# A hybrid decoder layer on one core: the state's chain ahead of the fourth attention block in the mixing stage

## What is computed

```python
h = rmsnorm(x, attn_norm_w); p = h @ w_in
q, k, v, p_rw = split(p)                      # 4 attention heads, 8 recurrent heads of 64
s = rope(q) @ rope(k).T * scale, causal       # two maps c for each attention head
p = softmax(s); a = p[0] - lam * p[1]
o_da = rmsnorm(a @ v, subln_w) * (1 - lam_init)
# recurrent group, state st of 64 x 64 for each head:
st = st * w_t - (st @ kk_t) * (kk_t * a_t) + v_t * k_t ;  y_t = st @ r_t
o_rw = (groupnorm(y) + bonus) * g
x = x + concat(o_da, o_rw) @ w_out
x = x + moe(rmsnorm(x))                       # top 4 of 32 experts, clamped SwiGLU
out = rmsnorm(x, final_norm_w)
```

## Time and profile before

| | |
|---|---|
| median of 3 runs | 1608.11 us (1607.88 to 1608.6) |
| the profiled execution's own time | 1607.04 us |
| its span | 1605.3 us |
| TensorE busy | 1544.0 us (96%) |
| VectorE busy | 1320.3 us (82%) |
| ScalarE busy | 1068.9 us (67%) |
| GpSimd busy | 324.7 us (20%) |
| DMA | 465.30 MB, mean 290 GB/s |

### The profile page before, as it was taken

One profiled execution on the slowest core, in us unless ns is written; L12 is line 12 of the kernel. 1 busy time (PEld: TensorE's weight loads), 2 busy tenths in 40 slices (PEclk: granted clock), 3 DMA queues, 4 the chain that ended last, 5 costly groups with the idle time before them and its releaser, 6 DMA issues.

```text
span 1605.3 us, 27281 instructions
## 1 busy us (share of the span) xinstructions
PE 1544.0 (96%) x10197; PEld 1253.3 (78%) x10198; DVE 1320.3 (82%) x1098; ACT 1068.9 (67%) x1011; POOL 324.7 (20%) x278
## 2 busy tenths in 40 slices
PE   5999999987899999999999999999999999999996
PEld 4777777765778888888888888888888888888885
DVE  5556565656498999999999999999999999999996
ACT  4635353434367777777777777777777777777774
POOL 6300000000145321122212211221122112212210
PEclk9999999998999999999999999999999999999998
DMA  6211111005399999999999999999999999999992
GB/s 191 63 54 41 55 41 54 15 2 215 157 391 367 373 395 385 382 380 374 376 372 381 388 384 374 376 367 376 373 386 382 379 373 376 371 371 381 381 377 114
DMA packets 98957, 465.30 MB, mean 290 GB/s; under 512 B 11392, under 2 KB 38048, under 8 KB 49616
## 3 DMA queue, kind: packets, MB, share of 16 engines
q1 hardware_dynamic: 86032, 429.59, 68.5%
q0 software_dynamic: 12864, 34.85, 8.3%
HBM read 448.51 MB, written 22.69 MB: 294 GB/s over the span
## 4 chain that ended last, share of the span: by engine, by line
PE 74%; DVE 1%; DMA 1%; issue 0%; ACT 0%; DVEq 0%; POOLq 0%
PE psum L1926 29%; PE psum L1929 14%; PE psum L1954 14%; PE psum L1959 7%; PE psum L1324 3%; PE psum L1908 2%; PE psum L1916 2%; PE psum L1942 1%; DVE w_pieces_lo L1748 0%; DMA xg<-h_rows,gath_i 0%; PE psum L2044 0%; PE psum L1340 0%; PE psum L1332 0%; DVE x L1870 0%; DMA w_pieces<-in_w_out 0%
## 5 line engine op out<-in xcount | busy, mean ns | idle before, releaser
L1748 DVE TENSOR_TENSOR w_pieces_lo<-w_pieces,w_pieces_hi 128x2048 fp32r<-128x2048 f32 x384 | 867.2, 2286 | 80.0 <-ACT w_pieces_hi L1612 79.9
L1612 ACT ACTIVATE w_pieces_hi<-w_pieces 128x2048 fp32r<-128x2048 f32 x384 | 736.1, 1919 | 220.4 <-PE psum L1929 156.3
L1926 PE MATMUL psum<-w_pieces_hi,xh 128*128 128x512 f32 x1024 | 284.4, 399 | 0.0
L1926 PE MATMUL psum<-w_pieces_hi,xl 128*128 128x512 f32 x1024 | 274.4, 390 | 0.0
L1929 PE MATMUL psum<-w_pieces_lo,xh 128*128 128x512 f32 x1024 | 274.2, 389 | 0.0
L1926 PEld LDWEIGHTS psum<-w_pieces_hi,xl 128*128 128x128 f32 x1024 | 192.2, 188 | 41.3
L1929 PEld LDWEIGHTS psum<-w_pieces_lo,xh 128*128 128x128 f32 x1024 | 192.2, 188 | 40.2
L1926 PEld LDWEIGHTS psum<-w_pieces_hi,xh 128*128 128x128 f32 x1024 | 185.4, 189 | 45.1 <-issue 11.3
L1552 POOL DMA_INDIRECT sum_rows<-ys,this_i x30 | 106.1, 3537 | 421.0 <-ACT ys L1632 420.7
L1954 PE MATMUL psum<-w_pieces_hi,ah 128*128 128x512 f32 x512 | 158.0, 390 | 0.1
L1954 PE MATMUL psum<-w_pieces_hi,al 128*128 128x512 f32 x512 | 157.7, 389 | 0.0
(11 more groups left out here) (366 smaller groups left out, 1893.2 us busy)
## 6 DMA issues: line engine op xcount, KB each, us to landing
w_pieces<-in_mlp_w SPq DMA_DIRECT2D x384, 1024.0 KB, 8.2
w_raw<-in_w_in SPq DMA_DIRECT2D x26, 512.0 KB, 4.0
w_pieces<-in_w_out SPq DMA_DIRECT2D x8, 512.0 KB, 9.3
sum_rows<-x POOLq DMA_DIRECT2D x5, 512.0 KB, 3.7
chunk_work<-in_x SPq DMA_DIRECT2D x4, 512.0 KB, 5.7
sc<-pall POOLq DMA_DIRECT2D x16, 128.0 KB, 3.8
x<-in_x SPq DMA_DIRECT2D x4, 512.0 KB, 13.8
h_rows<-w_pieces POOLq DMA_DIRECT2D x4, 512.0 KB, 2.9
```

The costliest lines, as they stand in the source:

```text
L1612: nc.scalar.activation(hi[:, p % RING], raw[:, raw_slot(b, p)].rearrange("p r n -> p (r n)"), ACT.Copy).then_inc(s_hi, 1)
L1748: nc.vector.tensor_tensor(lo[:, p % RING], raw[:, raw_slot(b, p)].rearrange("p r n -> p (r n)"), hi[:, p % RING].bitcast(F32), ALU.subtrac ...
L1926: nc.tensor.matmul(bank(up_bank(b) + c), a[:, k, :], hi[:, p % RING, c * 512:(c + 1) * 512], start=False, stop=False)
```

## The change

Three streams are reordered, and the three lists of names with them. Nothing is added and nothing is left out.

- ScalarE: `exponents(3)` comes behind the two copies e_wu0 and e_wu1 rather than ahead of them.
- VectorE: `weights(3)` comes behind z1 rather than ahead of L743.
- TensorE: `turn_weights(3)` comes behind `state(1)` and `y_within(0)` rather than ahead of them, and `output(3)` comes behind `state(3)` rather than ahead of `y_within(2)`.

```diff
--- before.py
+++ after.py
@@ -197,10 +197,10 @@
           + ["t2_0", "t2_1", "mr", "x2_0", "a_turn0", "x2_1", "o0", "score1"]
           + ["t3_0", "t3_1", "t_khat", "bonus", "x3_0", "a_turn1", "x3_1", "o1", "score2"]
           + ["t4_0", "t4_1", "t_v", "x4_0", "a_turn2", "x4_1", "o2", "akv", "score3"]
-          + ["wu0", "wu1", "q", "chunk", "a_turn3", "z1", "z2", "o3", "z3", "z4", "z5", "y_in", "z6", "o_turn", "y", "y_sum"])
+          + ["wu0", "wu1", "q", "chunk", "z1", "a_turn3", "z2", "z3", "o3", "z4", "z5", "y_in", "z6", "o_turn", "y", "y_sum"])
 MIX_ACT = (["sig_w", "kk_sq", "sig_a", "exps", "kk_log", "kk_norm", "grow", "keep", "gate", "e_kappa", "e_beta"]
            + ["exp0", "v_major", "a_major0", "o_copy0", "exp1", "e_khat", "a_major1", "o_copy1", "exp2", "e_v", "a_major2", "o_copy2"]
-           + ["e_akv", "exp3", "e_wu0", "e_wu1", "a_major3", "o_copy3", "o_log", "o_rs", "o_n", "gain", "y_sq", "y_log", "y_rs"])
+           + ["e_akv", "e_wu0", "e_wu1", "exp3", "a_major3", "o_copy3", "o_log", "o_rs", "o_n", "gain", "y_sq", "y_log", "y_rs"])
 MIX_DVE = (["mix_k", "kk0", "lsum", "mix_r", "mix_v", "kk",
             "kappa", "b", "beta", "rhat", "kmod", "khat"]
            + [f"{a}{h}" for h in range(2) for a in ("x1a", "x1b", "ea")]
@@ -208,7 +208,7 @@
               "ek0", "ek1", "max0"]
            + [n for lv in range(2, 5) for n in [f"et{lv}_0", f"et{lv}_1"] + [f"{a}{lv - 2}" for a in ("rl", "nl", "a")]
               + [f"ex{lv}_0", f"ex{lv}_1"] + [[], [], ["er"], ["bon", "shade"], []][lv] + [f"max{lv - 1}"]]
-           + ["rl3", "nl3", "a3", "eg", "eh", "e_q"] + [f"z{c}" for c in range(1, 8)]
+           + ["eg", "eh", "e_q", "z1", "rl3", "nl3", "a3"] + [f"z{c}" for c in range(2, 8)]
            + ["o_out", "y_n", "ot1", "ot2"])
 
 
@@ -511,10 +511,10 @@
             act.wait_ge(PE.sem, PE.reached(j, "akv"))
             nc.scalar.activation(rh[:, :, :, 64:128].rearrange("p h t c -> p (h t) c"),
                                  bank(2).rearrange("p (u c) -> p u c", c=64), ACT.Copy).then_inc(AC.sem, AC.step("e_akv"))
-            exponents(3)
             for h in range(2):
                 act.wait_ge(PE.sem, PE.reached(j, f"wu{h}"))
                 nc.scalar.activation(wu[:, h].rearrange("p t c -> p (t c)"), bank(3 * (1 - h)), ACT.Copy).then_inc(AC.sem, AC.step(f"e_wu{h}"))
+            exponents(3)
             weights_turned(3)
             output_copied(3)
             act.wait_ge(AC.sem, AC.reached(j, f"o_copy{NT - 1}"))
@@ -737,7 +737,6 @@
             largest(3)
             if more:
                 split(n0 + 6)
-            weights(3)
 
             dve.wait_ge(PE.sem, PE.reached(j, "chunk"))
             nc.vector.tensor_tensor(gt[:].rearrange("p (t c) k -> p c t k", c=2), psum[:, 0:2, 0:256].rearrange("p c (t k) -> p c t k", k=64),
@@ -752,6 +751,7 @@
                                     kr[:, :, 1, :].rearrange("p t (c k) -> p c t k", c=2), ALU.add).then_inc(DV.sem, DV.step("e_q"))
             own("eh")
             nc.vector.tensor_copy(zz[:, 1, :], hp[:, 0, :]).then_inc(DV.sem, DV.step("z1"))
+            weights(3)
             for c in range(1, 7):
                 dve.wait_ge(PE.sem, PE.reached(j, f"z{c}"))
                 nc.vector.scalar_tensor_tensor(zz[:, c + 1, :], bank(2, c * 64, c * 64 + 64), pe_[:, c, CH:CH + 1],
@@ -987,7 +987,6 @@
                                             start=False, stop=True)
             last.then_inc(PE.sem, PE.step("chunk"))
             fill(n0 + 4, 6, 8)
-            turn_weights(3)
 
             def y_within(u):
 
@@ -1008,11 +1007,12 @@
 
             state(1)
             y_within(0)
+            turn_weights(3)
             state(2)
             y_within(1)
-            output(3)
             y_within(2)
             state(3)
+            output(3)
             y_within(3)
             y_within(4)
             state(4)
```

## The result

The changed kernel takes 1612.3 us, the median of 16 runs (1610.51 to 1613.7), against 1607.98 us for the kernel before (16 runs): a ratio of 1.0026, with a 95% interval of 1.0019 to 1.0033. That is 4.3 us slower, over the 0.2% that can be told from no change. The forecast was 3.0 us slower, at 1611.1 us, with a range from 1607.9 to 1612.8. The profiled execution took 1610.51 us at a span of 1608.8, the fastest of the 16.

The account below looks back on a forecast made before the run. TensorE was taken to bound the kernel, 74% of the span, with the end of `front` passing delays on one to one. 3 x 0.91 + 0.30 = 3.0 us gave 1611.1 us from 1608.11, range 1607.9 to 1612.8.

Parts of the forecast that it names:

- forecast proper: Whole kernel: 3.0 us slower, own range 1610.3 to 1612.0 from 0.78 to 1.1 per turn and 0.1 to 0.5 in turn 4; chance 0.6.
- rival B: Turns 1 to 3: each pays unhidden tiling changes, 0.37 a turn, 1.1 in three; 4.1 us slower, 1612.2; chance 0.2.
- 373.2 foretold: Sign at the end of `front`: output projection loads (L1116) issued near 373.2, against 370.18 before.
- `q` earlier by 1.17 in turn 4: ScalarE's part in turn 4: with `wu` copied ahead of the exponentials, `q` starts at about 352.31 instead of 353.48.
- No gain in turns 1 to 3: ScalarE's part there brings nothing, since `q` starts behind tile slices after the last copy ends; z1 does not move.
- `am` 1.30 behind z1's start: VectorE's `weights(3)` between z1 and z2: `am` ready 1.30 us after z1's start, TensorE waiting and going on 0.06 later.
- 0.91 for each of turns 1 to 3: TensorE's part: state(4) starts 0.91 us later in each of turns 1 to 3, 2.7 in all.
- Nothing hides it: Next turn starts from y_sum behind 18 tile matmuls on TensorE, so the delay of turns 1 to 3 is passed on whole.
- +0.30 in turn 4: End of turn 4: the attention block, ready early before, becomes the late one; output(3) and y come 0.30 us later.
- 0.58 that I had used: TensorE's four transposes plus the way back to 64 x 64 pieces, ahead of state(2): 0.58 us.
- C: Absorbed: next turn waits for something not hanging on TensorE, giving back 0.91 per turn; only +0.30 stays, 1608.4; chance 0.13.
- A: Faster: the wait for `am` holds nobody, turns 1 to 3 cost nothing, turn 4 gives 1.17; 1606.9 us; chance 0.07.

Follow-up runs that it names:

- e1: The change made in turn 4 alone, turns 1 to 3 as in the kernel before: 1608.36 us against 1608.43 for the kernel before.
- e11: The kernel with the change in turn 4 alone, profiled a second time, one run: 1607.9 us.
- e3: The changed kernel plus ten idle-filling matmuls in TensorE's waits of turn 4: 1609.87 us against 1608.43 for the kernel before.
- e4: Only TensorE's order changed against the kernel before, ScalarE and VectorE left as they were: 1609.69 us against 1608.43.
- e6: Only ScalarE's order changed against the kernel before, copies of wu ahead of the exponentials: 1606.97 us against 1608.19.
- e9: The changed kernel unaltered, run for a third profile, one execution: 3120 us.
- e8: The kernel before plus five filling matmuls behind the transposes of turn 4: 1607.94 us against 1608.19 for the kernel before.
- e10: The changed kernel unaltered, run for a fourth profile, one run: 1612.04 us.
- e5: The changed kernel unaltered, measured again with a second profile: 1613.2 us against 1608.19 for the kernel before.

## Why the forecast came out as it did

The measured 1612.3 us lies in the stated range, but above the 1610.3 to 1612.0 of the forecast proper, and "slower by over 0.2%", which is what came, had the smaller chance (0.4 against 0.57 for no difference that can be told). The mechanism of the sum was right and gives 2.6 us; that the range held the rest too is luck, since it was stretched for rival B, and the term that filled it was in no rival. L1116 at 373.00 against the 373.2 foretold is luck as well: 1.7 us less ahead of the first `wu` and 1.9 more by turn 4's clock met there.

- **`q` earlier by 1.17 in turn 4**: right, 1.18. No gain in turns 1 to 3: right, z1 stands where it stood.
- **`am` 1.30 behind z1's start, and TensorE held by it**: right to 0.01. The transposes start 8.80 behind L967 in turn 1 (8.81 foretold), state(2) 9.38 (9.39), state(3) 10.10 (10.11), `output(3)` 10.37 (10.37).
- **0.91 for each of turns 1 to 3**: the mechanism was right and one term mis-sized, the two y_within behind `output(3)`. I took 0.4 from a stretch that held a wait; state(4) follows the output's end (124.80) by about 0.28. So the turn costs 0.78. Three of them: 2.3 instead of 2.7.
- **Nothing hides it**: right, the distances from y to the next `wu` are unchanged.
- **+0.30 in turn 4, since the attention block becomes the late one**: right where the clock holds, 13.98 and 13.97 (e1, e11, e3) against 13.67.
- **What failed** is a term that the sum did not have: TensorE's clock in turn 4. I costed the two waits there (2.1 us before the first state, 0.5 before the transposes) at their own length, because TensorE had nothing else to do. The turn cost up to 1.9 us more (15.83 against 13.98), through a clock of 0.50 in the stretch behind them, and filling them took that away (e3).
- **Rival B** (4.1 us) had the right size for the wrong reason: its changes of form would have shown as 1.28 in each of turns 1 to 3, and those took 0.78, of which e4 leaves 0.15 for the order. The drain at a change of tiling mode that the Trainium skill names (TensorEngine Tiling (Array Packing), Key Properties) was inside the 0.58 that I had used: state(2) came where it was foretold. **C** fell with the unchanged distances, **A** with the 0.56 that TensorE waits for `am`.

For the clock the Trainium skill has a rule, which I did not use: TensorE: Matmul & The Clock Gate, Part 1: The HAM clock gate, says that the array's clock is halved by default and that only activity lifts it. The fourth turn agrees in part: 0.50 behind idling and 1.00 in e3 with the same waits filled, but 1.00 too in e1 and e11 with the waits unfilled.

What stays open is why the same turn 4 lost its clock in three profiles of three in the changed kernel and in none of two in e1's. It starts 0.7 to 2.9 us earlier in e1's (`wu` at 349.57 and 349.37, against 350.30, 351.26 and 352.22), but the start alone doesn't decide: e4 and e6 lost the clock with `wu` at 349.42 and 349.65. Chance, with odds that differ from kernel to kernel, fits as well, and no run moved the new turn 4 alone. How many executions of the changed kernel lose the clock isn't known either. Their times, all 22 at 1610.5 us or more against a sum without it of about 1610.6, say that most do. The mean granted clock of each run points the same way: 0.9865 over these 22, and 0.9878 over e3's 11, which is 2.1 us of full clock less.

## What to carry to other kernels

Before an operation is moved into a chain of short round trips, look at what the chain's engines must do in order: VectorE's 1.2 us for the attention weights was free in its old place and became TensorE's wait in the new one. Where two pieces of work compete for one engine, try an idle other engine before a new order on the first: the copies of `wu` on VectorE brought z1 1.08 us forward, the new order on ScalarE 0.90. And a wait of TensorE in a stretch without filling work can cost more than its length, here up to 1.9 us more: price what follows it at half the clock as well, and try filling it.

## What the runs showed of the hardware

- The granted clock fell to 0.50 for up to 7 us behind short matmuls with waits between them (2.11 us the longest just before it in the changed kernel, 1.24 in e6), and not always: the same instructions kept 1.00 in e1 and e11. At 0.50 four transposes take 0.45 us more (1.11 against 0.66) and eight matmuls 0.9 more (2.07 against 1.16).
- A similar low clock at 59 to 63 us, behind a wait at the start of the first turn, shows in nine of thirteen profiles (e9 apart) and is missing in four (changed, e4, e8, e10). The wait is the same 2.48 us with it (before, e5) and without it (changed, e10). From the first turn's start to its `wu` it is 63.9 us with it and 62.3 without. Two profiles of one program (changed and e5) can so differ by 1.6 us in a place that no edit touched.
- One execution of the changed kernel (e9) took 3120 us. Its matmuls of the expert loop have a median of 713 ns against 389, from end to end, while its profile has no record of a clock below full:

```profile
L1926 PE MATMUL psum<-w_pieces_hi,xh x1024: 605/713/915, 779.3 to 3037.5; 128*128 128x512 f32 x171
```

  In the expert loop it starts 5049 matmuls in 2221 us (779 to 3000), one every 0.44 us. In the changed kernel's own profile 128x512 matmuls of 0.63 us start every 0.43 at 380 to 384 us, where the granted clock is 0.50. So e9 looks like the low clock throughout with no record of it, which is not shown. What held it back isn't in its trace, and no other run showed it.
